# Step 0 of a matrix-state recurrence, prepared inside the matrix product before it

## Chip, cores and metric

The kernel runs on one core of one Trainium2 chip. The metric is the device time of one execution in microseconds (us), as the median of several runs.

## What is computed

A trunk of two layers on 512 tokens of width 1024, in float32. Layer 0 has a gated mixer (gMLP), layer 1 an RWKV-7 time mixer; a squared-ReLU MLP and a LayerNorm follow each. The change lies in the time mixer of layer 1. Its projections come first, then a recurrence over tokens with a 64x64 state per head:

```python
r = xr @ w_rkv[0]
k = xk @ w_rkv[1]
v = xv @ w_rkv[2]
...
def step(state, inp):
    r_t, w_t, k_t, v_t, kk_t, b_t = inp
    sa = jnp.einsum('bhij,bhj->bhi', state, -kk_t)
    state = (state * w_t[:, :, None, :] + sa[..., None] * b_t[:, :, None, :]
             + v_t[..., None] * k_t[:, :, None, :])
    y = jnp.einsum('bhij,bhj->bhi', state, r_t)
    return state, y
```

The kernel doesn't run it token by token. It takes 128 tokens of 8 heads at once (a step), turns the decays into cumulated exponents, and gets the effect of the tokens in a step on each other from 128x128 products (the grams) and a triangular inverse.

## The kernel before

**Engines.** Five programs are written out by hand, one for each engine, and meet only in semaphores. Each engine works in the order in which its program is written, so an instruction that waits holds all that stands behind it.

**Products.** A float32 weight slab of 128 rows (`raw`) is split in two parts, `w_hi` by ScalarE and `w_lo` by POOL (GpSimd); the tokens likewise in `a_hi` (ScalarE) and `a_lo` (VectorE). `row_tile(j, t, ...)` does one slab `j` (one of 4 slots) for one token tile `t` (one of 4): six matmul instructions into banks 2t and 2t+1 of PSUM. `row_product` runs eight slabs: the first four slab by slab, the last four with the token tile as the outer loop, so that tile 0 is finished first and ScalarE can evict it (`projected`, by way of `stage` to the DRAM tensor `proj`) while the others are summed. `tile_summed` and `slab_used` tell of finished tiles and slabs, `proj_read` of evicted banks. The projections run in the order key, receptance, value. The sigmoids, keys and receptances of the first tokens come back from `proj` to `early` while the value product runs; the values (`late`) come after it.

**The recurrence.** Eight steps, each a pair of token tile and half of the heads (`Step(i)`). For each of them come, in this order: scaling and norm of kk; `log_decays` (TensorE: one product with the triangle `cumulate` into bank CUM, four with `halves` into bank HALVES); `decay_before` (VectorE: the exponent p_prev); `decays_of` (ScalarE: four exponentials); `decay_ab` and `decay_kr` (VectorE: four token products into `tok_ar` and `tok_bk`); `turn_ab` and `turn_rk` (TensorE: 16 transposes into four banks GRAM); `turned_pairs` (ScalarE: copies to `turned4`); `interactions(n, g)` (TensorE: the grams, in two halves g, into the same banks); `mask_grams` (VectorE: eight masks into `gram`); and then `iteration`, in which the inverse of step q is built while the state passes step s = q - 1 and step n = q + 1 is prepared. Step 0 has nothing to be prepared in: before, its preparation stands between the value product and the first `iteration`. On POOL, `scale_k` and `bonus_terms` prepare the keys and the bonus (`rk`).

**Memory.** The buffers of the recurrence lie over those of the products: `gram`, `inverse` and `k_rest` over weight slots and operands, `start` over an end of `big`. So `inverse` and `k_rest` can only be written when the value product is done; VectorE waits for that with `slab_used`, then clears `inverse`, makes `k_rest` and clears `start` (semaphore `zeroed`), and builds `select`, `terms` and a column of `block_inv` from the identity.

Of the kernel before, what the change touches and what calls it, by code (L numbers as in the profile page):

```python
# [6 lines left out]
P = 128  # L7
# [45 lines left out]
def trunk(nc, x, ln1_g, ln1_b, ln2_g, ln2_b, ffn_w1, ffn_w2, gm_w_in, gm_vn_g, gm_vn_b, gm_ws, gm_bs,  # L53
# [7 lines left out]
    HALF = D // 2  # L61
# [34 lines left out]
    with ExitStack() as ctx:  # L96
# [92 lines left out]
        turned4 = over("turned4", [P, 2, PAIRS, 4, P])  # L189
        kkn, scratch, k_gain = (over(name, [P, HALF]) for name in ("kkn", "scratch", "k_gain"))  # L190
# [83 lines left out]
        GRAM = (2, 3, 5, 6)  # L274
        TURN_BANK = (0, 1, 4, 5, 6, 0, 1, 7)
# [114 lines left out]
        def _(pool):  # L390
# [164 lines left out]
        def _(act):  # L555
# [183 lines left out]

            products = ("key", "receptance", "value")  # L740
# [12 lines left out]
            for u, name in enumerate(products):  # L753
# [11 lines left out]
                for t in range(TT):  # L765
# [8 lines left out]
                    projected(3 + u, t, ACT.Copy)  # L774


            def decays_of(n):

                act.wait_ge(lx_ready, n.nth(1, 1))
                nc.scalar.activation(decays[:, n.i % 3], bank[HALVES][:, 0:2 * PAIRS].rearrange("p (a b) -> p a b", b=2),  # L780
                                     ACT.Exp).then_inc(exp_ready, 1)
                nc.scalar.activation(p_prev[:], p_prev[:], ACT.Exp).then_inc(exp_ready, 1)
                nc.scalar.activation(p_inv[:], bank[CUM][:], ACT.Exp, scale=-1.0).then_inc(exp_ready, 1)
                nc.scalar.activation(p_mid[:], bank[CUM][:], ACT.Exp).then_inc(exp_ready, 1)
# [35 lines left out]
            def copy_corner(q):  # L820

                act.wait_ge(level_summed, q.nth(6, 6))
                if q.i >= 2:
# [47 lines left out]
            def turned_pairs(n):  # L871
                for p in range(PAIRS):
                    act.wait_ge(turned_summed, n.nth(PAIRS, p + 1))
                    nc.scalar.activation(turned4[:, n.half, p].rearrange("p a t -> p (a t)"), bank[GRAM[p]][:],
                                         ACT.Copy).then_inc(turned_ready, 1)

# [984 lines left out]
```

## Time and profile before

| | |
|---|---|
| median of 3 runs | 1432.93 us (1430.86 to 1434.05) |
| the profiled execution | 1430.15 us, span 1428.4 us |
| TensorE (PE) | busy 1342.5 us, 94% of the span |
| VectorE (DVE) | 675.5 us, 47% |
| ScalarE (ACT) | 512.0 us, 36% |
| GpSimd (POOL) | 589.3 us, 41% |
| mean granted clock of TensorE | 0.963 |

The busy shares are averages over the whole kernel. The value product ends at about 733 us and the recurrence lies between there and about 1010 us; the rest is products. The profiled execution is not one of the three runs of the median.

### The profile page before, as it was taken

Reading aid. Unit: us, or ns where it says so; the run is one execution under the profiler, and the core shown is the slowest. Engines: PE = TensorE matmul, PEld = TensorE weight load, DVE = VectorE, ACT = ScalarE, POOL = GpSimd, SP = SyncE. Lnnn points to the kernel's source line nnn. Section 1 sums busy time; section 2 is a strip of 40 time slices with the busy share of each in tenths; the row PEclk is TensorE's granted clock in tenths of the full one; section 3 lists DMA queues with packets and bytes.
Section 4 is the critical chain, followed back from the end, with each engine's and each line's share of the span. In section 5 each row is a group of like instructions: output and inputs, shape, how many; then the busy total and the mean of one; then the engine's idle time right before and its main releaser. Section 6 shows DMA issues by size and latency. Waiting matters only on the chain.

```text
span 1428.4 us, 22922 instructions
## 1 busy us (share of the span) xinstructions
PE 1342.5 (94%) x9193; PEld 1087.4 (76%) x9193; DVE 675.5 (47%) x871; ACT 512.0 (36%) x879; POOL 589.3 (41%) x356
## 2 busy tenths in 40 slices
PE   7989999999999979999977999998799999999996
PEld 6878888888888852477755888777678888888885
DVE  2475811112444485146647677772582111244447
ACT  4443232223232321433433666765323322323230
POOL 4344344444444450134524354553344444344440
PEclk9999999999999989999988989998899999999999
DMA  7224243333443330534531111101234333233321
GB/s 265 74 74 133 74 120 101 93 97 103 130 124 97 98 102 16 193 116 148 177 133 31 32 46 47 46 20 59 84 107 120 102 91 100 77 114 103 91 71 59
DMA packets 108974, 138.22 MB, mean 97 GB/s; under 512 B 6162, under 2 KB 81986, under 8 KB 108900
## 3 DMA queue, kind: packets, MB, share of 16 engines
q1 hardware_dynamic: 104292, 120.37, 28.0%
q10 hardware_dynamic: 4608, 16.78, 3.1%
q8 instruction: 56, 0.92, 0.3%
q14 instruction: 18, 0.15, 0.0%
HBM read 122.45 MB, written 14.68 MB: 96 GB/s over the span
## 4 chain that ended last, share of the span: by engine, by line
PE 76%; DVE 17%; ACT 4%; issue 2%; POOL 0%; DMA 0%; ACTq 0%; SPq 0%; DVEq 0%; POOLq 0%
PE bank L1402 35%; PE bank L1455 8%; PE bank L1454 8%; PE bank L1456 8%; DVE a_lo L983 3%; PE bank L1547 2%; PE bank L1564 2%; DVE gram L1263 2%; DVE x_tok L1011 2%; DVE x_tok L1009 2%; PE bank L1753 1%; DVE stats L1000 1%; PE bank L1637 1%; DVE x_tok L1026 1%; DVE v_tok L1011 1%
## 5 line engine op out<-in xcount | busy, mean ns | idle before, releaser
L397 POOL TENSOR_TENSOR w_lo<-raw,w_hi 128x1024 fp32r<-128x1024 f32 x184 | 454.9, 2478 | 644.7 <-ACT w_hi L569 636.7
L569 ACT ACTIVATE w_hi<-raw 128x1024 fp32r<-128x1024 f32 x184 | 193.6, 1056 | 292.2 <-PE bank L1402 280.5
L1402 PE MATMUL bank<-w_hi,a_hi 128*128 128x512 f32 x896 | 280.3, 394 | 16.1 <-DVE a_lo L983 11.0
L1402 PE MATMUL bank<-w_lo,a_hi 128*128 128x512 f32 x896 | 277.6, 391 | 0.0
L1402 PE MATMUL bank<-w_hi,a_lo 128*128 128x512 f32 x896 | 277.0, 390 | 0.0
L1454 PE MATMUL bank<-xT_hi,w_hi 128*128 128x512 f32 (+1 forms) x640 | 236.1, 369 | 0.0
L1455 PE MATMUL bank<-xT_lo,w_hi 128*128 128x512 f32 (+1 forms) x640 | 235.5, 368 | 0.0
L1456 PE MATMUL bank<-xT_hi,w_lo 128*128 128x512 f32 (+1 forms) x640 | 235.4, 368 | 0.0
L983 DVE TENSOR_TENSOR a_lo<-big,a_hi 128x512 fp32r<-128x512 f32 x64 | 140.6, 2202 | 182.6 <-ACT a_hi L588 179.5
L1402 PEld LDWEIGHTS bank<-w_hi,a_hi 128*128 128x128 f32 x896 | 166.8, 189 | 57.6 <-issue 16.0
L1402 PEld LDWEIGHTS bank<-w_lo,a_hi 128*128 128x128 f32 x896 | 169.1, 189 | 35.7
L1402 PEld LDWEIGHTS bank<-w_hi,a_lo 128*128 128x128 f32 x896 | 168.9, 189 | 35.7
L1092 DVE TENSOR_TENSOR big<-relu 128x512 f32 (+1 forms) x64 | 45.6, 712 | 274.6 <-ACT relu L696 274.6
L1454 PEld LDWEIGHTS bank<-xT_hi,w_hi 128*128 128x128 f32 x640 | 120.7, 189 | 20.1
L1456 PEld LDWEIGHTS bank<-xT_hi,w_lo 128*128 128x128 f32 x640 | 120.7, 189 | 20.1
L1455 PEld LDWEIGHTS bank<-xT_lo,w_hi 128*128 128x128 f32 x640 | 120.7, 189 | 19.5
L696 ACT ACTIVATE relu<-bank 128x512 f32<-128x512 f32 x64 | 38.4, 600 | 236.2 <-PE bank L1456 236.2
L983 DVE TENSOR_TENSOR a_lo<-mix,a_hi 128x512 fp32r<-128x512 f32 x24 | 43.1, 1795 | 83.4 <-ACT a_hi L744 83.4
L1263 DVE TENSOR_TENSOR gram<-bank,keep_before 128x512 f32<-128x512 f32 x64 | 39.0, 680 | 15.7 <-PE bank L1617 15.7
L727 ACT ACTIVATE stage<-bank 128x512 f32<-128x512 f32 x48 | 26.0, 594 | 55.6 <-PE bank L1402 40.5
L473 POOL COPY inverse<-grown 32x256 f32<-32x256 f32 x32 | 17.3, 539 | 62.1 <-issue 35.4
L1617 PE MATMUL bank<-turned 64*128 64x256 f32 x256 | 39.3, 409 | 0.0
(219 smaller groups left out, 1435.0 us busy)
## 6 DMA issues: line engine op xcount, KB each, us to landing
raw<-in_ffn_w SPq DMA_DIRECT2D x128, 512.0 KB, 3.9
raw<-in_rw_w_rkv SPq DMA_DIRECT2D x24, 512.0 KB, 3.6
proj<-stage ACTq DMA_DIRECT2D x24, 512.0 KB, 2.6
raw<-in_gm_w_in SPq DMA_DIRECT2D x16, 512.0 KB, 4.3
early<-proj SPq DMA_DIRECT2D x8, 1024.0 KB, 6.1
raw<-in_gm_w_out SPq DMA_DIRECT2D x8, 512.0 KB, 3.6
raw<-in_rw_w_o SPq DMA_DIRECT2D x8, 512.0 KB, 3.5
late<-proj SPq DMA_DIRECT2D x8, 512.0 KB, 3.9
```

The lines of the kernel that those rows point to most:

```text
L397: nc.gpsimd.tensor_tensor(w_lo[:, j, :], raw[:, j, :], w_hi[:, j, :].bitcast(F32), ALU.subtract).then_inc(w_lo_ready, 1)
L569: nc.scalar.activation(w_hi[:, j, :], raw[:, j, :], ACT.Copy).then_inc(w_hi_ready, 1)
L696: nc.scalar.activation(relu[:, j % 2, :], bank[j][:], ACT.Relu).then_inc(bank_read, 1)
L983: nc.vector.tensor_tensor(a_lo[:, j, :], source(i * SLOTS + j), a_hi[:, j, :].bitcast(F32), ALU.subtract).then_inc(a_lo_ready, 1)
L1011: nc.vector.scalar_tensor_tensor(y, y, rstd[:, 0:1], gains[:, 1, :], ALU.mult, ALU.add).then_inc(result, 1)
L1092: nc.vector.tensor_tensor(big[:, i * SLOTS + j, :], relu[:, j % 2, :], relu[:, j % 2, :], ALU.mult).then_inc(squared, 1)
L1263: nc.vector.tensor_tensor(gram[:, n.half, h:h + 3:2, 2 * g:2 * g + 2, :], bank[GRAM[b]][:].rearrange("p (e a t) -> p e a t", e=2, a=2), ke ...
L1402: last = nc.tensor.matmul(bank[2 * t + h][:], a[:, j, tok], w[:, j, h * HALF:(h + 1) * HALF], start=start and a is a_hi and w is w_hi, sto ...
L1454: nc.tensor.matmul(dst, w_hi[:, j, col], xT_hi[:, k, tokens], start=k == 0, stop=False)
L1455: nc.tensor.matmul(dst, w_hi[:, j, col], xT_lo[:, k, tokens], start=False, stop=False)
L1456: last = nc.tensor.matmul(dst, w_lo[:, j, col], xT_hi[:, k, tokens], start=False, stop=k == KT - 1)
L1617: last = nc.tensor.matmul(bank[GRAM[b]][:, p % 2 * 2 * P:(p % 2 + 1) * 2 * P], turned4[r, n.half, p, (B_, K_)[g], :], turned4[r, n.half, p ...
```

## The change

Step 0 of the recurrence is prepared inside the value product. `row_product` calls a function `between(t, j)` after each row tile of its last four slabs, and for the value product TensorE does there: the log decays after row tile (1,0), `turn_ab` after (2,1), `turn_rk` after (2,3), the first half of the grams after (3,1), and the second after (3,3), the last. For step 0 the banks differ: 0 and 1 for the decays and 0 to 3 for transposes and grams, which are the banks of token tiles 0 and 1, once they have been evicted. ScalarE gets the exponentials behind the eviction of tile 0 and the copies of turned pairs behind that of tile 2; VectorE masks the first half before it waits for the end of the value product. Since `p_prev`, `p_inv` and `p_mid` lie over memory that the product still uses, step 0 has three buffers of its own in the second half of `turned4`. `k_rest` and the clearing of `start` and `inverse` go to POOL, which waits for the end of the value product; TensorE now waits for `zeroed` ahead of the first `iteration` and no longer ahead of the transposes. Waits for the last stores to `proj` go to where a buffer that lies over `stage` is first written (`copy_xa`, `centre_y`).

```diff
+        p_prev0, p_inv0, p_mid0 = (sb(name, [P, HALF], at=place["turned4"] + (PAIRS * 4 * P + m * HALF) * 4)
+                                   for m, name in enumerate(("p_prev0", "p_inv0", "p_mid0")))
...
+        def gram_banks(n):
+            return GRAM if n.i else (0, 1, 2, 3)
+
+        def decay_banks(n):
+            return (CUM, HALVES) if n.i else (0, 1)
+
+        def exponents(n):
+            return (p_prev, p_inv, p_mid) if n.i else (p_prev0, p_inv0, p_mid0)
...
             scale_k(Step(0))
+
+            pool.wait_ge(slab_used, first_slab["rw_out"])
+            then(nc.gpsimd.tensor_scalar(k_rest[:], k_a[:], -1.0, 1.0, ALU.mult, ALU.add))
+            then(nc.gpsimd.memset(start[:], 0.0))
+            nc.gpsimd.memset(inverse[:], 0.0).then_inc(zeroed, 1)
             for z in range(2):
...
                     projected(3 + u, t, ACT.Copy)
+                    if name == "value" and t == 0:
+                        decays_of(Step(0))
+                    if name == "value" and t == 2:
+                        turned_pairs(Step(0))
...
             def copy_xa(s):
+                if s.i == 0:
+                    for z in range(2):
+                        act.wait_ge(stage_out[z], 16 * 6 * TT // 2)
...
-            decays_of(Step(0))
-            for z in range(2):
-                act.wait_ge(stage_out[z], 16 * 6 * TT // 2)
-            turned_pairs(Step(0))
             steps(iteration)
...
             decay_kr(first_step)
+            mask_grams(first_step, 0)
 
             dve.wait_ge(slab_used, first_slab["rw_out"])
-            then(nc.vector.memset(inverse[:], 0.0))
-            then(nc.vector.tensor_scalar(k_rest[:], k_a[:], -1.0, 1.0, ALU.mult, ALU.add))
-            nc.vector.memset(start[:], 0.0).then_inc(zeroed, 1)
             then(nc.vector.tensor_reduce(select[:], ident[:].rearrange("p (m j) -> p j m", j=BASE), AX.X, ALU.add))
             for c in range(BASE):
                 here = select[:, c:c + 1].broadcast_to([P, HH])
                 then(nc.vector.tensor_copy(terms[:, :, c, c], here))
                 if c == 0:
                     then(nc.vector.tensor_copy(block_inv[:, :, 0], here))
-            for z in range(2):
-
-                dve.wait_ge(stage_out[z], 16 * 6 * TT // 2)
-            mask_grams(first_step)
+            mask_grams(first_step, 1)
             steps(iteration)
...
+            def within_value(t, j):
+
+                if (t, j) == (1, 0):
+                    pe.wait_ge(masks_ready, 1)
+                    pe.wait_ge(proj_read, 8 * 5 + 2)
+                    log_decays(first_step)
+                if (t, j) == (2, 1):
+                    pe.wait_ge(proj_read, 8 * 5 + 4)
+                    turn_ab(first_step)
+                if (t, j) == (2, 3):
+                    turn_rk(first_step)
+                if (t, j) == (3, 1):
+                    interactions(first_step, 0)
+                if (t, j) == (3, 3):
+                    interactions(first_step, 1)
+            for u, name in enumerate(("key", "receptance", "value")):
+                row_product(name, KT, None, lambda t: pe.wait_ge(proj_read, 8 * (u + 2) + 2 * t + 2),
+                            between=within_value if name == "value" else None)
...
-            pe.wait_ge(proj_read, 8 * 5 + 6)
-            log_decays(Step(0))
             pe.wait_ge(proj_read, 8 * 6)
             pe.wait_ge(zeroed, 1)
-            turn_ab(Step(0))
-            turn_rk(Step(0))
-            interactions(Step(0), 0)
-            interactions(Step(0), 1)
             steps(iteration)
```

On ScalarE, from the last operands of the value product on, before (stage is the eviction, turned_101 is `turned4`):

```order
L738 ACTIVATE small<-small 128x8 [waits ss_ready]
L727 ACTIVATE stage<-bank 128x512 [waits stage_out0,tile_summed]
L727 ACTIVATE stage<-bank 128x512
L730 DMA proj<-stage 128x1024 [waits proj_read]
L727 ACTIVATE stage<-bank 128x512 [waits stage_out1,tile_summed]
...
L780 ACT_TABLE_LOAD
L780 ACTIVATE decays<-bank 128x8 [waits lx_ready]
...
L874 ACTIVATE turned_101<-bank 128x512 [waits turned_summed,stage_out1,stage_out0]
L874 ACTIVATE turned_101<-bank 128x512 [waits turned_summed] x3
```

and now:

```order
L754 ACTIVATE small<-small 128x8 [waits ss_ready]
L743 ACTIVATE stage<-bank 128x512 [waits stage_out0,tile_summed]
L743 ACTIVATE stage<-bank 128x512
L746 DMA proj<-stage 128x1024 [waits proj_read]
L761 ACT_TABLE_LOAD
L761 ACTIVATE decays<-bank 128x8 [waits lx_ready]
...
L770 ACTIVATE turned_101<-bank 128x512 [waits turned_summed] x4
L743 ACTIVATE stage<-bank 128x512 [waits stage_out1,slab_used]
```

The exponentials have moved ahead of the evictions of tiles 1 to 3, and the copies of turned pairs ahead of that of tile 3.

On VectorE, from the last token product of step 0 to its masks, before:

```order
L1207 TENSOR_TENSOR tok_ar<-early,p_mid 128x512 [waits exp_ready]
L1347 MEMSET inverse 128x1024 [waits slab_used]
L1348 TENSOR_SCALAR k_rest<-k_a 128x1024 [waits dve_done]
L1349 MEMSET start 128x1024 [waits dve_done]
L1350 TENSOR_REDUCE select<-ident 128x8
L1353 COPY terms<-select 128x8 [waits dve_done]
L1355 COPY block_inv<-select 128x8 [waits dve_done]
L1353 COPY terms<-select 128x8 [waits dve_done] x7
L1263 TENSOR_TENSOR gram<-bank,keep_before 128x2x256 [waits stage_out1,gram_summed,stage_out0,dve_done]
L1263 TENSOR_TENSOR gram<-bank,keep_before 128x2x256 [waits gram_summed] x7
```

and now (the last group is the second half of the masks):

```order
L1229 TENSOR_TENSOR tok_ar<-early,p_mid_104 128x512 [waits exp_ready]
L1289 TENSOR_TENSOR gram<-bank,keep_before 128x2x256 [waits gram_summed] x4
L1375 TENSOR_REDUCE select<-ident 128x8 [waits slab_used]
L1378 COPY terms<-select 128x8 [waits dve_done]
L1380 COPY block_inv<-select 128x8 [waits dve_done]
L1378 COPY terms<-select 128x8 [waits dve_done] x7
L1289 TENSOR_TENSOR gram<-bank,keep_before 128x2x256 [waits gram_summed,dve_done]
L1289 TENSOR_TENSOR gram<-bank,keep_before 128x2x256 [waits gram_summed] x3
```

The three large instructions have left VectorE, and half of the masks stand ahead of the wait for the last slab. On POOL the three stand now between the last product of `scale_k` and the first of `bonus_terms`:

```order
L502 TENSOR_TENSOR early<-early,k_gain 128x512 [waits k_linked]
L557 TENSOR_SCALAR k_rest<-k_a 128x1024 [waits slab_used]
L558 MEMSET start 128x1024 [waits pool_done]
L559 MEMSET inverse 128x1024 [waits pool_done]
L517 TENSOR_TENSOR rk<-early 128x512 [waits early_in0,k_ready,stage_out1,stage_out0]
```

Before, the first of these was followed at once by the last.

## Rows read from the trace of the kernel before

**Rows 1.** The page: busy us, share of the span and instructions of each engine.

```profile
PE 1342.5 (94%) x9193; PEld 1087.4 (76%) x9193; DVE 675.5 (47%) x871; ACT 512.0 (36%) x879; POOL 589.3 (41%) x356
```

**Rows 2.** The chain that ended last, 714 to 760 us: start us, us, what.

```profile
732.87 1.10 ACT stage L727 x2
...
734.34 1.28 ACT L780
...
741.15 0.92 DVE inverse L1347
...
743.07 0.92 DVE start L1349
...
749.51 4.88 DVE gram L1263 x8
754.53 1.10 PE bank L1583 x2
...
756.41 0.98 PE bank L1629 x2
```

**Rows 3.** Timeline of TensorE: start us, us, what, and the idle time before it.

```profile
717.70 0.62 PE L1402 MATMUL bank<-w_hi,a_hi 128*128 128x512 f32 x2
...
732.67 1.02 PE L1583 MATMUL bank<-early,cumulate 128*128 128x512 f32 x2
733.53 0.95 PE L1585 MATMUL bank<-halves,early 128*128 128x2 f32 x8
744.09 0.45 PE L1595 MATMUL bank<-ident,tok_ar 128*128 128x128 f32 x1 [9.61 <-DVE start L1349]
...
747.66 5.51 PE L1617 MATMUL bank<-turned 64*128 64x256 f32 x32
```

**Rows 4.** Windows of TensorE: us, busy (instructions), granted clock, DMA share, GB/s.

```profile
738.00:739.00 1.00, 0.00 (x0) 0.82 0.92 190
...
748.00:749.00 1.00, 1.00 (x7) 0.56 0.08 16
749.00:750.00 1.00, 1.00 (x12) 1.00 0.00 0
...
759.00:760.00 1.00, 0.00 (x0) 0.56 0.00 0
```

**Rows 5.** Timeline of ScalarE: eviction, table load, copies of turned pairs.

```profile
717.41 1.07 ACT L727 ACTIVATE stage<-bank 128x512 f32<-128x512 f32 x2
...
734.34 1.28 ACT L780 ACT_TABLE_LOAD   x1 [0.39 <-ACT stage L727]
...
746.57 2.06 ACT L874 ACTIVATE turned<-bank 128x512 f32<-128x512 f32 x4 [9.27 <-PE bank L1603]
```

**Rows 6.** Timeline of VectorE.

```profile
719.80 1.66 DVE L1188 SCALAR_TENSOR_TENSOR scratch<-kkn,early 128x512 f32<-128x512 f32 x1
...
736.97 1.75 DVE L1199 TENSOR_TENSOR tok_bk<-scratch,p_inv 128x512 f32<-128x512 f32 x1
...
744.60 1.43 DVE L1353 COPY terms<-select 128x8 f32<-128x8 f32 x7
...
823.32 0.77 DVE L1182 TENSOR_SCALAR small<-small 128x8 f32<-128x8 f32 x1
```

**Rows 7.** Timeline of POOL at two of these places.

```profile
736.75 1.43 POOL L506 TENSOR_TENSOR rk<-early 128x512 f32<-128x512 f32 x1 [15.83 <-DMA proj<-stage]
...
822.80 1.26 POOL L509 TENSOR_TENSOR rk<-rk,r_k 128x512 f32<-128x512 f32 x1
```

**Rows 8.** A transpose at full clock (timeline), and grams of step 1 (chain).

```profile
772.76 0.28 PE L1603 MATMUL bank<-ident,tok_ar 128*128 128x128 f32 x1
772.88 0.27 PE L1603 MATMUL bank<-ident,tok_bk 128*128 128x128 f32 x1
...
773.78 1.11 PE bank L1617 x8
```

**Rows 9.** Groups of POOL's instructions: busy us, mean ns of one, idle before.

```profile
L397 POOL TENSOR_TENSOR w_lo<-raw,w_hi 128x1024 fp32r<-128x1024 f32 x184 | 454.9, 2478 | 644.7 <-ACT w_hi L569 636.7 <-PE bank L1753 8.0
...
L409 POOL TENSOR_SCALAR_AFFINE_SELECT ws_in<-ws_in 128x1024 f32<-128x1024 f32 x1 | 1.1, 1089 | 0.0
...
L423 POOL MEMSET keep_before<- 128x256 f32 x1 | 0.3, 318 | 0.0
```

**Rows 10.** Line 1182 on VectorE: ns min/median/max of its eight instructions.

```profile
L1182 DVE TENSOR_SCALAR small<-small x8: 128/130/772, 717.5 to 943.1; 128x8 f32<-128x8 f32 x8
```

More of the change, by code:

```diff
@@ L738, in norm_of, with decays_of, turned_pairs @@
                 nc.scalar.activation(small[:, NORM, :], small[:, SQ, :], ACT.Sqrt).then_inc(norm_ready, 1)
+            def decays_of(n):
+                prev, inv, mid = exponents(n)
+                cum, halves_bank = decay_banks(n)
+                act.wait_ge(lx_ready, n.nth(1, 1))
+                nc.scalar.activation(decays[:, n.i % 3], bank[halves_bank][:, 0:2 * PAIRS].rearrange("p (a b) -> p a b", b=2),
+                                     ACT.Exp).then_inc(exp_ready, 1)
+                nc.scalar.activation(prev[:], prev[:], ACT.Exp).then_inc(exp_ready, 1)
+                nc.scalar.activation(inv[:], bank[cum][:], ACT.Exp, scale=-1.0).then_inc(exp_ready, 1)
+                nc.scalar.activation(mid[:], bank[cum][:], ACT.Exp).then_inc(exp_ready, 1)
+            def turned_pairs(n):
+                for p in range(PAIRS):
+                    act.wait_ge(turned_summed, n.nth(PAIRS, p + 1))
+                    nc.scalar.activation(turned4[:, n.half, p].rearrange("p a t -> p (a t)"), bank[gram_banks(n)[p]][:],
+                                         ACT.Copy).then_inc(turned_ready, 1)
             products = ("key", "receptance", "value")
@@ L774, in _ @@
                     projected(3 + u, t, ACT.Copy)
[L777 to L784, printed above, removed]
+                    if name == "value" and t == 0:
+                        decays_of(Step(0))
+                    if name == "value" and t == 2:
+                        turned_pairs(Step(0))
             def copy_diagonal(q):
@@ L822, in copy_corner @@
                 act.wait_ge(level_summed, q.nth(6, 6))
+                act.wait_ge(zeroed, 1)
                 if q.i >= 2:
@@ L1176, in decay_before @@
                 dve.wait_ge(cum_summed, n.nth(1, 1))
-                nc.vector.scalar_tensor_tensor(p_prev[:], early[:, n.half, SIG, :], -DECAY, bank[CUM][:],
+                nc.vector.scalar_tensor_tensor(exponents(n)[0][:], early[:, n.half, SIG, :], -DECAY, bank[decay_banks(n)[0]][:],
                                                ALU.mult, ALU.add).then_inc(lx_ready, 1)
@@ L1198, in decay_ab @@
                     dve.wait_ge(s_summed, n.i - 2)
-                nc.vector.tensor_tensor(tok_bk[:, n.i % 3, 0, :], scratch[:], p_inv[:], ALU.mult).then_inc(tok_ready, 1)
+                nc.vector.tensor_tensor(tok_bk[:, n.i % 3, 0, :], scratch[:], exponents(n)[1][:], ALU.mult).then_inc(tok_ready, 1)
             def decay_kr(n):
@@ L1228, in centre_y @@
             def centre_y(s):
+                if s.i == 0:
+                    for z in range(2):
+                        dve.wait_ge(stage_out[z], 16 * 6 * TT // 2)
                 dve.wait_ge(y_summed, s.nth(1, 1))
@@ L1256, in link, with mask_grams @@
                 dve.wait_ge(base_linked, q.nth(LINKS + len(LEVELS), k))
-            def mask_grams(n):
-                for k in range(2 * PAIRS):
-                    b, g = k % PAIRS, k // PAIRS
+            def mask_grams(n, g):
+                for b in range(PAIRS):
+                    k = g * PAIRS + b
                     h = b // 2 * 4 + b % 2
@@ L1407, in row_product @@
             def row_product(name, count, turning=None, bank_free=None, split_turns=False,
-                            first_tiles=range(TT), begun=False):
+                            first_tiles=range(TT), begun=False, between=None):
                 n0, m0 = first_slab[name], first_act[name]
@@ L1441, in row_product @@
                             turn_x(turning, t - 2)
+                        if between is not None:
+                            between(t, j)
                     if t < TT - 1:
@@ L1567, in _ @@
                     last.then_inc(bank_projected, 1)
-            for u, name in enumerate(("key", "receptance", "value")):
-                row_product(name, KT, None, lambda t: pe.wait_ge(proj_read, 8 * (u + 2) + 2 * t + 2))
-            pe.wait_ge(masks_ready, 1)
             def head(ap, h):
```

28 lines of the change are left out of this document (13 added, 15 removed).

## Prediction

> **What bounds the kernel now.** I read the page first: TensorE is busy for 94% of the span [rows 1], so the kernel is matmuls with gaps, and a change that moves work pays only where it fills a gap on TensorE's path. The chain of waits, read in order of time, shows the one gap that this change can reach [rows 2]. The value product ends at 732.67, where TensorE goes over to the log decays of step 0 without a wait [rows 3]. Then the chain leaves TensorE: ScalarE's eviction, its table load and its exponential, four token products on VectorE, and then three VectorE instructions from 741.15 to 744.0 that clear two buffers and make k_rest. TensorE sits idle for 9.61 us until the last of them is done [rows 3]. After it come 16 transposes, 32 instructions of grams, and eight masks that end at 754.39, on which the log decays of step 1 wait [rows 2, 3]. So from 732.67 to 754.53 TensorE has 21.9 us, of which only 1.8 (log decays), 3.6 (transposes) and 5.5 (grams, paced by the masks) are work. I then read the engines one by one over this stretch, and the windows for the clock: the granted clock is 1.00 until 738, falls to 0.50 during the wait, stays there to 748, is back at 1.00 at 749, and falls again at about 759.5, some two microseconds into the next wait [rows 4]. The 16 transposes, from 744.09 to near 747.6 [rows 3], ran at 0.21 us apiece at the lower level.
>
> **The change, step by step.** I follow TensorE from the middle of the value product.
>
> Hook (1,0), the log decays. They stand after the first row tile of token tile 1, which ends at 717.70 [rows 3]; they write banks 0 and 1, so they wait for ScalarE's two copies of token tile 0, which end at 717.41 + 1.07 = 718.5 [rows 5]. That is a wait of 0.9 us with hand-over, a new one: ScalarE is late there because of the root and its table load. Behind it on TensorE stand all remaining row tiles. The work itself is 1.8 us (732.67 to 734.48, [rows 3]); it was on the path before too.
>
> Exponentials and token products. VectorE is free for the exponent of step 0 when scratch ends, 719.80 + 1.66 = 721.5 [rows 6], after the log decays are there (720.4). Then 0.7 us for it, four exponentials in 1.7 us (the table load of 1.28 us [rows 5] starts behind the eviction at 718.9 and is over by 720.2, hidden under the wait), and the products with p_prev, p_inv, p_inv, p_mid. They took 0.69 us alone but 1.75 where POOL's rk product ran [rows 6, 7]; POOL has nothing to do between 720.9 and the end of the value product, so I take 0.7 each, and the last is done at about 726. ScalarE is free again at 724, before token tile 1 ends at 724.4, so no eviction is late.
>
> Hook (2,1) and (2,3), the transposes. Token tile 1 ends at 717.70 + 0.9 + 1.8 + 3 x 1.36 = 724.4, two row tiles of tile 2 (eleven of them lie between 717.70 and 732.67 [rows 3], so 1.36 us each) take it to 727.2; tokens and evictions are there by 726, so no wait. Sixteen transposes at full clock, 0.12 us each as at 772.76 [rows 8], are 1.9 us in place of 3.6.
>
> Hook (3,1), the first half of the grams. It starts at 734.5. Its operands are ScalarE's four copies (2.06 us [rows 5]), which follow the eviction of tile 2 (730.9 to 732.0) and its store, and end at 734.4: a margin of 0.1 us, so up to 0.5 us may be lost here. The first eight of such instructions took 1.11 us in the next step [rows 8], so sixteen are 2.2; half of the mask-paced 5.51 [rows 3], 2.75, is the upper bound and 1.7 the lower. The four masks run under the last two row tiles.
>
> The value product thus ends at 732.67 + 0.9 + 1.8 + 1.9 + 2.2 = 739.5.
>
> After it. TensorE runs the second half of the grams (2.2 us) and is done at 741.7. Their masks stand on VectorE behind select and nine small copies, which wait for the last value slab, as POOL's three new instructions do. On VectorE these small ones took 2.1 us, from the end of start at 743.99 to 746.03, the last seven of them 1.43 [rows 2, 6]. POOL: the memsets have a row at 256 columns (0.318) and, at 1024 columns, the affine select (1.089) stands nearest [rows 9]; I take 1.0 us for a memset and 1.1 for k_rest, bounded by 0.7 (VectorE's own) and by POOL's 2.5 for a two-input product of this width [rows 9], and 3.3 us for all three with their links, from 739.6 to 742.9. This is where the two engines meet. A one-input VectorE instruction of 128x8 took 0.77 us where POOL ran a product, and its end at 824.09 is that product's (822.80 + 1.26); alone its shortest is 0.13 [rows 6, 7, 10]. The copies have the same size and also one input, in SBUF, so I take it that they are held up: about two slip in between POOL's three, and seven run after 742.9, to 744.35. Four masks of 0.61 (eight in 4.88, [rows 2]) end at 746.8, against 754.4 before. Gain so far 7.6 us. POOL's zeroed, for which TensorE now waits ahead of step 1, is there at 742.9, before the masks, so it costs nothing in itself; it would from 746.8 on.
>
> The rule behind this in the Trainium skill (SBUF — State Buffer, section "SBUF: two separate sides") is that the port pair which VectorE and GpSimd share is an exclusive lock for a whole instruction, which a VectorE instruction in a two-port mode needs against any GpSimd instruction. It speaks against this change, since it lets even a memset hold the copies; by it the masks end at 746.8, and no row of before shows a memset beside a copy.
>
> The clock. TensorE is idle from 741.7 to 746.8, 5.1 us. Before, the clock fell 4.3 us into the wait from 734.5, and about two into the one from 757.4 [rows 4], so I expect half speed when the log decays of step 1 and the replication start, which before ran at full clock from 754.53 to 757.4 [rows 2, 4]. Two pairs of 128x512 instructions (0.43 us apiece) double: 1.7 us, and the eight small ones 0 to 0.8; I take 2.1 in all. That is given back from the gain.
>
> Everything behind is moved as a whole: rk on POOL follows the store of the last value tile (before, 2.8 us from the end of the eviction, 732.87 + 1.10, to the start of rk at 736.75 [rows 2, 7]) and lies at 743.6 to 746.3, the level products on POOL have over 2 us of room, the loads of late and early have more. The sum is 7.6 - 2.1 = **5.5 us faster**. The profiled execution is 1430.15 us, which gives 1424.6; it lies 2.8 us below the median of the runs shown, so on that scale 1427.4.
>
> **Rivals** (times on the scale of the median).
> - As above, but the clock holds (the phase of the wait is luckier): 7.6 us, 1425.3. For it: the wait is new in length and place. Against it: both waits of this length in the rows lost the clock. 15%.
> - The copies aren't held up (they may not need what the 128x8 instruction needed, and the memsets read nothing). They end at 741.7, the masks at 744.1, 10.3 us earlier; rk at 743.6 then meets in_block and spread, as the 1.75 us product [rows 6] met it, and takes 0.7 back: 9.6, 1423.3, or 7.5 if the clock falls in this shorter wait. 20%.
> - The hooks stall or POOL is slow: k_rest at 2.5 us in place of 1.1 costs 1.4 more, the copies for turned 0.5, the grams 0.6; that leaves about 3 us, 1430. 11%.
> - No change within what can be told: ends above cancel further, or the time comes back in the recurrence, whose clock follows its own waits. 6%.
> - Slower, by one mechanism: the clearing on POOL. TensorE's wait for zeroed decides once the three instructions end after 746.8. With the clock's 2.1 us the gain is gone when they end at 752.3, which asks for 12.7 us in place of 3.3, or k_rest alone at 10.5 us; slower by over 0.2% needs 2.9 us more. POOL's 2.5 us for two inputs of this width [rows 9] speak against it; that no one-input arithmetic of this kind on POOL stands in the trace speaks for it. At 18 us in all it would be 5.3 us slower, 1438.2. 3%.
>
> **How the numbers follow.** The first case has 45%, with a range of its own of 1426 to 1429. A difference of 0.2% (2.9 us) is about what a measurement of this kernel can tell from none; the three runs shown spread over 3.2 us. The range reaches from the unheld copies with some luck (gain 10.4, 1422.5) to the stalled case (gain 2.7, 1430.2), and leaves out about 1 in 10 on the slow side and little on the fast. Faster by over 0.2%: 88%; within: 9%; slower: 3%.
>
> **What would show it.** In the profile after: TensorE idle by 0.9 us before the log decays at about 717.7; transposes of 0.12 us between row tiles at clock 1.00; no wait before the first grams; value ending near 739.5; POOL's k_rest, start, inverse in about 3.3 us; the small copies on VectorE, one or two of them near 1 us long; the last mask near 746.8; step 1's log decays at clock 0.50 with 0.85 us for an instruction. I am wrong if the copies end by 742 or the clock is 1.00 there (more gain), or if TensorE waits for zeroed or tokens (less).

## The result and the profile after

The changed kernel takes 1419.34 us in the median of 4 runs (1417.69 to 1421.46), the kernel before 1432.13 in the same comparison (4 runs, 1430.86 to 1434.05). The ratio is 0.9914, with a 95% interval of 0.9895 to 0.9933. That is 12.8 us, more than twice the 5.5 that was forecast, and the time lies below the range (1422.5 to 1430.2).

The page of the profiled execution (1419.39 us) begins:

```profile
span 1417.6 us, 22925 instructions
...
PE 1333.8 (94%) x9193; PEld 1078.0 (76%) x9193; DVE 674.6 (48%) x868; ACT 512.5 (36%) x879; POOL 591.5 (42%) x359
```

The number of TensorE's instructions is that of [rows 1], but their busy time is 8.7 us shorter. The work hasn't shrunk; the same instructions ran faster. This is the first sign of where most of the gain lies.

First, the place of the change. The timeline of TensorE after (columns as in [rows 3]):

```profile
719.18 1.10 PE L1604 MATMUL bank<-early,cumulate 128*128 128x512 f32 x2 [0.72 <-issue]
...
727.88 0.27 PE L1616 MATMUL bank<-ident,tok_ar 128*128 128x128 f32 x1
727.98 0.27 PE L1616 MATMUL bank<-ident,tok_bk 128*128 128x128 f32 x1
...
735.21 2.00 PE L1638 MATMUL bank<-turned 64*128 64x256 f32 x16
740.12 2.00 PE L1638 MATMUL bank<-turned 64*128 64x256 f32 x16
748.27 2.05 PE L1604 MATMUL bank<-early,cumulate 128*128 128x512 f32 x2 [6.15 <-DVE gram L1289]
750.11 1.71 PE L1606 MATMUL bank<-halves,early 128*128 128x2 f32 x8
751.68 2.05 PE L1671 MATMUL bank<-spread,keep_block 128*128 128x512 f32 x2
```

This execution reached the value product 0.6 us later than the one of before. Less that, the value product ends at 739.5, as worked out: a wait of 0.72 us, transposes at 0.11 us apiece, no wait ahead of the first grams, whose sixteen instructions took 2.0 us. Then TensorE waits 6.15 us for the masks, and the log decays and the replication (the product of spread, the last row above) run at half speed (0.50 granted, the 1.2 GHz level): 5.5 us from 748.27 to the end of the replication, where before it was 2.9 [rows 2]. VectorE and POOL in this wait:

```profile
736.37 2.48 DVE L1289 TENSOR_TENSOR gram<-bank,keep_before 128x512 f32<-128x512 f32 x4 [10.37 <-PE bank L1638]
...
740.65 0.71 DVE L1378 COPY terms<-select 128x8 f32<-128x8 f32 x1
741.39 0.98 DVE L1380 COPY block_inv<-select 128x8 f32<-128x8 f32 x1
742.41 3.20 DVE L1378 COPY terms<-select 128x8 f32<-128x8 f32 x7
745.64 2.48 DVE L1289 TENSOR_TENSOR gram<-bank,keep_before 128x512 f32<-128x512 f32 x4
```

```profile
740.28 1.04 POOL L557 TENSOR_SCALAR k_rest<-k_a 128x1024 f32<-128x1024 f32 x1 [18.82 <-PE bank L1424]
741.39 0.96 POOL L558 MEMSET start<- 128x1024 f32 x1
742.40 0.96 POOL L559 MEMSET inverse<- 128x1024 f32 x1
...
744.11 1.26 POOL L517 TENSOR_TENSOR rk<-early 128x512 f32<-128x512 f32 x1 [0.75 <-DMA proj<-stage]
745.44 1.28 POOL L520 TENSOR_TENSOR rk<-rk,r_k 128x512 f32<-128x512 f32 x1
```

Read the ends against each other: the copy of 741.39 ends at 742.37, when start is cleared (742.35). The next waits for inverse (743.36), and one more for rk (745.37). The two memsets and the product hold the copies alike, each one copy: four of the nine took 0.7 to 1.1 us, the other five 0.17 to 0.18. The last mask ends at 748.12, and the replication of step 0 starts at 751.68 in place of 756.27, 4.6 us earlier. Only that much is won here.

The rest comes later. A step lasts from one replication (line 1629 before, 1671 after) to the next; below are these distances as worked out from the starts of the replication's rows, and in brackets the time at half clock within each (a low stretch is a time at half clock).

| us | step 0 | 1 | 2 | 3 | 4 | 5 | 6 | last replication |
|---|---|---|---|---|---|---|---|---|
| before | 26.85 (13.7) | 30.75 (6.8) | 30.88 (6.8) | 31.08 (6.8) | 28.16 (0) | 29.55 (3.4) | 30.70 (6.8) | 964.24 |
| after | 29.41 (21.7) | 27.93 (0) | 28.02 (0) | 29.50 (3.4) | 28.28 (0) | 29.62 (3.4) | 27.75 (0) | 952.19 |

The windows over steps 1 to 6 (columns as in [rows 4]), before and then after:

```profile
783.10:964.20 181.10, 169.35 (x3232) 0.92 0.13 38
```

```profile
781.10:952.20 171.10, 159.31 (x3233) 0.98 0.13 40
```

The same instructions, one record apart, took 10.0 us less under a granted clock of 0.98 than under 0.92. The sum, in the times of the two traces: 4.6 us up to the first replication, less 2.6 given back in step 0, which lay at half clock for 21.7 us, plus 10.0 in the six steps behind, makes 12.05 at the last replication. 1.2 of it is lost again in the products behind, so that the spans differ by 10.8. A group of instructions in step 1 shows how: the same 16 products (y_rest) lie in a low stretch before and outside one after.

```profile
792.49 3.01 PE L1753 MATMUL bank<-us,gram 128*128 128x64 f32 x16 [0.19 <-ACT us L812]
795.43 1.08 PE L1637 MATMUL bank<-grown_t,level_m 32*32 32x32 f32 x64
```

```profile
790.47 2.00 PE L1795 MATMUL bank<-us,gram 128*128 128x64 f32 x16 [0.46 <-ACT us L843]
792.39 0.75 PE L1679 MATMUL bank<-grown_t,level_m 32*32 32x32 f32 x64
```

### The profile page after: what moved, and what is told of

It is laid out like the page before. It is cut to its first block, busy times and chain, and to the rows that moved or that the text cites. A ratio compares the mean times of both kernels' runs of the same rounds, so it can differ in the third digit from the quotient of the medians.

```text
span 1417.6 us, 22925 instructions
## 1 busy us (share of the span) xinstructions
PE 1333.8 (94%) x9193; PEld 1078.0 (76%) x9193; DVE 674.6 (48%) x868; ACT 512.5 (36%) x879; POOL 591.5 (42%) x359
## 4 chain that ended last, share of the span: by engine, by line
PE 76%; DVE 17%; ACT 4%; issue 2%; POOL 0%; DMA 0%; SPq 0%; DVEq 0%; ACTq 0%; POOLq 0%
PE bank L1424 35%; PE bank L1480 8%; PE bank L1478 8%; PE bank L1479 8%; DVE a_lo L1005 3%; PE bank L1571 2%; PE bank L1588 2%; DVE gram L1289 2%; DVE x_tok L1033 2%; DVE x_tok L1031 2%; DVE stats L1022 1%; PE bank L1679 1%; PE bank L1795 1%; DVE x_tok L1048 1%; DVE v_tok L1033 1%
## 5 line engine op out<-in xcount | busy, mean ns | idle before, releaser
L484 POOL COPY inverse<-grown 32x256 f32<-32x256 f32 x32 | 17.3, 539 | 52.0 <-issue 28.2
```

## Experiments

Two theories stand against each other. **C** (clock): the steps are shorter after the change only because the low stretches fall elsewhere. **O** (order): something in the steps is released earlier, and the clock follows from it. A separate question is what holds the copies.

| kernel | median us (range, runs) | ratio to before, 95% interval |
|---|---|---|
| b_late1 | 1428.58 (1424.83 to 1430.03, 10) | 0.9978 (0.9968 to 0.9988) |
| b_late2 | 1432.85 (1431.49 to 1434.48, 10) | 1.0006 (0.9995 to 1.0018) |
| a_late1 | 1426.53 (1424.36 to 1433.21, 10) | 0.9966 (0.9948 to 0.9984) |
| a_fill | 1423.41 (1419.28 to 1431.91, 10) | 0.9938 (0.9923 to 0.9952) |
| a_again | 1424.19 (1418.64 to 1426.65, 6) | 0.9918 (0.9889 to 0.9947) |
| a_third | 1420.50 (1417.55 to 1424.41, 6) | 0.9909 (0.9887 to 0.9931) |
| b_pool | 1425.23 (1423.44 to 1429.74, 9) | 0.9941 (0.9922 to 0.9960) |
| a_dve | 1430.25 (1424.26 to 1434.53, 12) | 0.9973 (0.9952 to 0.9993) |
| a_order | 1426.51 (1417.58 to 1432.82, 12) | 0.9947 (0.9923 to 0.9971) |
| a_act | 1421.05 (1415.49 to 1426.24, 6) | 0.9922 (0.9896 to 0.9949) |
| a_act2 | 1420.67 (1410.95 to 1425.01, 6) | 0.9914 (0.9884 to 0.9945) |
| b_keep | 1429.27 (1427.48 to 1431.06, 12) | 0.9979 (0.9967 to 0.9991) |
| a_keep | 1426.52 (1424.88 to 1430.21, 12) | 0.9966 (0.9955 to 0.9977) |
| b_pool_keep | 1425.99 (1424.05 to 1429.58, 6) | 0.9947 (0.9926 to 0.9968) |
| a_dve_keep | 1426.51 (1424.26 to 1427.66, 6) | 0.9948 (0.9928 to 0.9968) |
| a_act2_keep | 1418.33 (1416.57 to 1419.92, 5) | 0.9890 (0.9869 to 0.9912) |

The kernel before had medians of 1431.97 to 1433.47 in these comparisons, over 11 to 31 runs each.

### A later start: b_late1, b_late2, a_late1

In b_late1 one more memset stands ahead of step 0's transposes, in b_late2 two:

```diff
             then(nc.vector.memset(inverse[:], 0.0))
+            then(nc.vector.memset(inverse[:], 0.0))
```

> The kernel before with one more memset of inverse (0.9 us, about 1.0 with its link) ahead of step 0's transposes, so that the whole recurrence starts 1.0 us later. Theory C (clock): the 7 to 8 us that the changed kernel gained between the first and the last step come from where the stretches at half clock fall in the steps. Then this delay doesn't simply add: the steps after the first change from their 30.7 to 31.1 us to some other length between 27.8 and 31, and the time can come out several us away from +1, likely below 1432. Theory O (order): the changed kernel's steps are shorter because something in them is released earlier (loads of early and late, POOL). Then this kernel keeps steps of about 30.8 us and is 1.0 us slower than before: ratio 1.0007.

> As b_late1 with two more memsets, about 2.0 us. Theory O: +2.0 us, ratio 1.0014, steps of 30.8 us. Theory C: not additive; with the shift of 1.4 us between the changed kernel's second step and a return of the same place of the clock, this or b_late1 should lose the lock of a low stretch in each step, with steps near 28 us and a time up to 7 us below before.

```diff
+            for _ in range(4):
+                then(nc.vector.memset(in_block[:], 0.0))
             mask_grams(first_step, 1)
```

> The changed kernel with four small memsets (128x256, together about 1.1 us) on VectorE ahead of the second half of step 0's masks. Theory O: 1.1 us slower than the changed kernel, 1420.4, steps as in it (27.8 to 29.6 us). Theory C: not additive; step lengths change, the time can lie anywhere between 1418 and 1428.

More work gave 4.1 us less (b_late1 against the 1432.68 of its comparison), then nothing (b_late2). In a_late1 the four memsets took 1.5 us, not 1.1, and the changed kernel became 2 to 7 us slower (against its three medians; 7 to 8 us by the ratios to before). b_late1 speaks against O, whose +1.0 us lies outside its interval; b_late2's interval holds both O's 1.0014 and no change, and a_late1 is only clearly above O's value against two of the three medians. In b_late1 steps 3 to 6 took 28.6, 29.5, 28.2 and 29.2 us in place of 31.1, 28.2, 29.6 and 30.7; b_late2 has the lengths of before within about 0.1 us in its steps 1 to 6. I had expected b_late2 too to lose the pattern, and it didn't; the regular return in the clock that its expectation supposes is borne out by no run. The delays weren't the round ones either: counted from the first matmul of the value product, the first replication came 0.6 us later than before in b_late1 and 2.75 us later in b_late2, where it ran at half clock.

### Idle products in the wait: a_fill

```diff
+            pe.wait_ge(early_in[1], 16)
+            for _ in range(6):
+                nc.tensor.matmul(bank[Y_BANK][:], ident[:], early[:, 1, SIG, :], start=True, stop=True)
             pe.wait_ge(zeroed, 1)
             steps(iteration)
```

> The changed kernel with six idle products (ident by early, 128x512 in float32, 0.86 us each at full clock, into a bank that isn't used yet) on TensorE between the evicted last tile and the log decays of step 1, where it waits 6.15 us for the masks. Nothing of the result uses them. Both theories: the clock is 1.00 at these log decays, which with the replication take 2.7 us in place of 5.5, so the local gain grows by 2.5 to 3 us. Theory O: the total falls by the same, to 1416.5. Theory C: the total moves by that and by whatever the steps behind do, so it may differ from 1416.5 by several us either way.

The first replication came at 748.5 in place of 751.7, as both theories said, but the total didn't fall: 0.9938 of before, where the changed kernel has 0.9909 to 0.9918. Its profiled execution, the slowest of the ten at 1431.91 us, had five steps running of 30.7 to 31.1 us with 6.8 us at half clock each.

### The changed kernel again: a_again, a_third

> The changed kernel once more, unedited, for its spread: its first four runs lie between 1417.7 and 1421.5. Theory C (clock): where the low stretches fall differs from one execution to the next, so more runs reach up to about 1430, with a median up to 5 us above 1419.3. Theory O (order): all runs within 2 us of 1419.3.

> The changed kernel unedited, a third set of runs. If its clock is better than that of before on average: median 1419 to 1424, about 10 us below before, in this set too. If the first sets were lucky: a median within 5 us of before, 1427 or more.

Sixteen runs in three comparisons lie between 1417.55 and 1426.65, with medians of 1419.3, 1424.2 and 1420.5. a_third's steps are those of the table above within about 0.1 us. a_again's trace is another: the same program, with the same 62.8 us from the first matmul of the value product to the first replication, took 176.9 us for steps 1 to 6, with 6.8 us at half clock in steps 1 and 4 (30.9 and 31.1 us) and 3.4 in steps 3 and 6. So the runs vary with the clock's pattern, as C says, and not with the order. The good pattern is the changed kernel's usual one (eleven of the sixteen runs lie at 1421.7 or below, the other five at 1423.9 to 1426.7), and the gain of about 12 us (9 in a_again's comparison) is no accident of the first four.

The traces without idle products in the steps say the same together. Their 78 steps 1 to 6, of both kernels and their variants, took 30.3 to 31.1 us with 6.8 us at half clock (37 steps), 29.1 to 29.8 with 3.4 (16) and 27.8 to 28.4 with none (21); only four steps 3 without one took 28.6 to 29.2. The length follows the low stretches, whichever the kernel.

The runs give a second estimate of the clock's share, since each has its mean granted clock. At 0.964, for instance, the changed kernel has three at 1423.9 to 1424.5, and before has three of 1429.3 on average. A straight line with one slope through the 16 runs of the changed kernel and the 91 of before puts the changed kernel 5.7 us lower at the same clock (standard error 0.4); the rest of the 12 goes with its higher clock, 0.968 against 0.961.

### Idle products in every step: b_keep, a_keep

```diff
+            def idle_product(q):
+                nc.tensor.matmul(bank[GRAM[3]][:], ident[:], gram[:, q.half, 0].rearrange("p a t -> p (a t)"),
+                                 start=True, stop=True)
...
                 level_left(q, 0)
                 if s:
+                    idle_product(q)
                     u_bottom(s)
+                    idle_product(q)
```

> The kernel before with two idle products (128x512 in float32, 0.86 us each, into a bank that is free there) in each of the seven later iterations, around u_bottom, ahead of the place where its low stretches begin. They change no result. They cost at most 1.7 us a step. Theory C: if they are enough to keep the clock, steps 2 to 8 have no low stretch and take 28 + 1.7 = 29.7 us each or less, all alike, so the seven steps take about 208 us as without them, and the time is within 3 us of before. Theory O: steps stay at 30.8 us and grow by up to 1.7: the seven steps take 216 to 220 us, 8 to 12 us slower.

> The changed kernel with the same two idle products per iteration. Theory C: its steps are then as long as those of b_keep, with or without, and the difference of the two kernels is what the change brought up to the first replication, 4 to 5 us. Theory O: the changed kernel's steps stay shorter than b_keep's by 1 us or more each and the difference is 10 to 13 us.

These two decide. The windows over steps 1 to 6 of b_keep, and then of a_keep:

```profile
783.70:959.30 175.60, 168.89 (x3257) 1.00 0.13 39
```

```profile
779.90:955.60 175.70, 168.61 (x3256) 1.00 0.13 39
```

There is no low stretch in either, and they take 175.6 and 175.7 us: where the clock holds, the change did nothing to these steps. b_keep's six steps are 5.5 us shorter than before's 181.1 although they hold twelve products more; a_keep's are 4.6 us longer than the changed kernel's 171.1. The kernels differ by 2.75 us in the median (by 2.3 in the mean of 12 runs each, with a standard error of 0.6), and by 3.7 in the two traces at the last replication: 6.4 at the first (756.8 and 750.4), less 2.6 in step 0 (26.85 and 29.44 us, with 13.7 and 21.8 at half clock, where no idle product stands). Of the 6.4, 1.2 is no gain: a_keep's execution reached the value product that much earlier. From there on it is 5.2 at the first replication, as in the changed kernel, and 2.5 at the last. O is refuted. I had expected a difference of 4 to 5; it is less, since step 0 takes part of it back.

### What holds the copies: a_dve, b_pool, a_order, a_act

a_dve moves the three clearing instructions back to VectorE, ahead of select. b_pool is the kernel before with them on POOL, behind `scale_k(Step(0))`, and with a wait of ScalarE for zeroed in `iteration`.

> The changed kernel with the clearing back on VectorE, ahead of select and the copies (2.8 us there), nothing of it on POOL. Held-up theory (POOL's three instructions and rk hold the small copies): the seven copies take 1.4 us again in place of 3.2, but 2.8 us of clearing are before them, so the last mask ends at most 0.6 us earlier or later than in the changed kernel (748.1): moving the clearing to POOL brought nothing by itself. Rival (the copies are slow for another reason, such as the buffers' place): the seven copies stay at 3.2 us and the last mask ends 2.8 us later. The median differs from the changed kernel's by whatever the clock does, up to 5 us.

> The kernel before with only the clearing moved to POOL, where in the changed kernel it stands. The transposes wait for zeroed and for the last token product (741.0 before), no longer for VectorE's clearing (744.0). POOL clears from about 733 to 736, under the exponentials, so the transposes start at 741.2 in place of 744.1 and the first replication 2.9 us earlier, at 753.4, if select and the copies don't hold the masks. Theory C: median anywhere from 1425 to 1433, since the steps behind depend on the clock; theory O: 1429.8.

The seven copies in a_dve and POOL beside them, and the seven in b_pool:

```profile
744.52 3.44 DVE L1377 COPY terms<-select 128x8 f32<-128x8 f32 x7
...
744.68 1.26 POOL L517 TENSOR_TENSOR rk<-early 128x512 f32<-128x512 f32 x1 [22.64 <-DMA proj<-stage]
746.02 1.28 POOL L520 TENSOR_TENSOR rk<-rk,r_k 128x512 f32<-128x512 f32 x1
```

```profile
741.87 1.44 DVE L1355 COPY terms<-select 128x8 f32<-128x8 f32 x7
```

In a_dve the numbers are near the rival's: the copies took 3.44 us without a clearing on POOL, and the last mask ended at 750.5, 2.4 us later than in the changed kernel, of which 0.6 is a later arrival at the value product. But the reason isn't the buffers' place: being later, the copies ran into rk (POOL, 744.68 to 747.30), which my expectation had left out. In b_pool the clearing (733.04 to 736.12) and rk (to 739.97) are over before the copies, and they took 1.44. The same buffers, so their place is out: POOL work beside the copies holds them, clearing or not, and where POOL is quiet they are quick. b_pool's first replication starts at 752.05, 0.4 us behind the changed kernel's 751.68 (0.9 from the value product on), with one of the change's parts.

a_order puts the second half of the masks ahead of select and the copies behind spread and the scaling of kk:

```diff
+            mask_grams(first_step, 1)
             dve.wait_ge(slab_used, first_slab["rw_out"])
             then(nc.vector.tensor_reduce(select[:], ident[:].rearrange("p (m j) -> p j m", j=BASE), AX.X, ALU.add))
-            for c in range(BASE):
...
-            mask_grams(first_step, 1)
             steps(iteration)
```

> The changed kernel with another order on VectorE: the second half of step 0's masks first, then the wait for the last value slab and select, and the nine small copies behind spread and the scaling of step 1's kk. The masks no longer stand behind the copies that POOL holds. The last mask ends about 4 us earlier (744 in place of 748.1), the log decays of step 1 start after 2 us of idle time in place of 6.15 and run at full clock, and the first replication starts between 746.5 and 749 in place of 751.7. Theory O: 3 to 5 us faster than the changed kernel. Theory C: the first replication moves so, the median by that and up to 5 us either way.

Masks end at 743.9 and the log decays of step 1 start at 744.04 at full clock, as expected. But the nine copies now lie beside the level products and `scale_k` and take 5.7 us, and step 0 took 35.2 us in place of 29.4. It was also at half clock for 27.3 us in place of 21.7; how much of the 5.8 us is the copies' and how much the clock's isn't told apart. The traced execution (1419.57) is one of the fast ones; the median is 1426.5. The last seven copies:

```profile
749.33 4.31 DVE L1342 COPY terms<-select 128x8 f32<-128x8 f32 x7
```

a_act gives the copies to ScalarE, with select made early:

```diff
+            def fill_terms():
+                act.wait_ge(select_ready, 1)
+                for c in range(BASE):
+                    here = select[:, c:c + 1].broadcast_to([P, HH])
+                    last = nc.scalar.activation(terms[:, :, c, c], here, ACT.Copy)
+                    if c == 0:
+                        last = nc.scalar.activation(block_inv[:, :, 0], here, ACT.Copy)
+                last.then_inc(terms_ready, 1)
...
                 copy_diagonal(q)
+                if q.i == 0:
+                    fill_terms()
```

> The changed kernel with select made early on VectorE and the nine small copies (terms, block_inv) on ScalarE behind the diagonals of step 0, where ScalarE waits. VectorE has nothing between the two halves of the masks. Held-up theory (any instruction of POOL holds such copies on VectorE): the copies take 0.2 us or less apiece on ScalarE though POOL runs beside them, the last mask ends near 743.9 and the first replication starts at 746 to 747 as in a_order, but the second follows after 27 to 30 us and not after 35. Rival (the copies are slow wherever they stand): they take over 3 us on ScalarE too. Total: 4 to 5 us below the changed kernel (1424 in the call before), by what the clock adds or takes, up to 5 us.

ScalarE's copies in a_act:

```profile
743.05 0.22 ACT L908 ACTIVATE terms<-select 128x8 f32<-128x8 f32 x1
743.17 0.20 ACT L910 ACTIVATE block_inv<-select 128x8 f32<-128x8 f32 x1
743.27 0.79 ACT L908 ACTIVATE terms<-select 128x8 f32<-128x8 f32 x7
```

They followed each other every 0.1 us. POOL's clearing had ended by then (742.95), but its rk product ran from 743.69 to 744.96, beside the last three of them, and they took 0.20 us like the others: the rival that they are slow anywhere is out, and a product on POOL doesn't hold them on ScalarE. That a memset on POOL wouldn't is not shown. The first replication starts at 745.6, and step 0 is 27.5 us long. The profiled execution then had 6.8 us at half clock in five of its six steps 1 to 6, which took 182.7 us in place of the changed kernel's 171.1, more than had been won. The median, 0.9922 of before, is no better than the changed kernel's.

### Apart from the clock: a_act2, b_pool_keep, a_dve_keep, a_act2_keep

a_act2 is a_act with `(t, j) == (1, 1)` in place of `(1, 0)` for the log decays; the kernels with keep have the idle products of b_keep.

> As a_act, and the log decays of step 0 stand one row tile later, behind (1,1). The wait of 0.72 us ahead of them goes away, tokens are ready 1.4 us later but before (2,1). The value product ends 0.7 us earlier than in a_act, with everything behind it, if the copies of turned pairs still end in time: total 0.7 us below a_act apart from the clock.

> b_pool (only the clearing moved to POOL) with the two idle products per iteration. In the profile of b_pool the first replication came 4.2 us earlier than before. If its step after that is as long as before's, the time is 1425 to 1426, level with a_keep (1426.5) or below it, and the clearing alone is worth as much as the whole change apart from the clock. If its first step is longer because the clock is low in it, 1428.

> a_dve (hooks in the value product, clearing on VectorE) with the idle products. Its first replication came 2.3 us later than the changed kernel's. Its first step was shorter, 27.5 against 29.4, so I expect 0 to 2.5 us above a_keep: 1427 to 1429.

> a_act2 (copies on ScalarE, log decays one row tile later) with the idle products. Its first replication came 7 to 8 us ahead of the changed kernel's, its first step was no longer. I expect 6 to 8 us below a_keep: 1418.5 to 1420.5, the best of this group; only 3 us if the gain is given back in the first step by the clock.

In a_act2 the log decays follow without a wait, and the first replication comes 1.3 us earlier than in a_act, counted from the first matmul of the value product. Its median is level with a_act's, and its six runs go from 1410.95, at a mean granted clock of 0.976, to 1425.01, at 0.961: 14 us in one kernel, by the clock.

Against b_keep's 1429.3, the clearing alone on POOL is worth 3.3 us (b_pool_keep), the hooks alone (the parts of step 0's preparation inside the value product) 2.8 (a_dve_keep), both together 2.8 (a_keep). Only a_keep stands in the same comparison as b_keep; by the ratios to before they are 4.6, 4.4 and 1.9 us, so these figures are good to about 2 us. The traces, counted from the first matmul of the value product, show it more sharply. The gains at the first replication are 4.1, 3.5 and 5.2 us: they don't add, since both parts shorten the same wait and together they meet in the held copies. Step 0, partly at half clock, takes back 0.9, 3.0 and 2.6 us of them. With the copies freed and the log decays one tile later it is 10.9 us (a_act2_keep; 12.7 by the ratios), and its steps 1 to 6 run without a low stretch:

```profile
774.80:950.30 175.50, 168.63 (x3256) 1.00 0.13 39
```

a_act2_keep is faster than before, at 0.9890 (0.9869 to 0.9912). Its median is 1.0 to 5.9 us below the three of the changed kernel, but the intervals overlap (in the same comparison a_third has 0.9909, 0.9887 to 0.9931), so that it beats the changed kernel isn't shown.

## Why the prediction was wrong

**What held.** The walk through the value product came out to 0.1 us (739.5), term by term: the wait at the first hook 0.72 for 0.9, log decays 1.8, transposes 1.8 for 1.9, grams 2.0 for 2.2. The clearing on POOL took 3.1 us for 3.3 and held the copies, as the 128x8 row of [rows 6] suggested; TensorE didn't wait for zeroed. Half clock at step 1's log decays came, as forecast. (The fall at "about 759.5" in the prediction is at 759.1 by its own row [rows 4], 0.56 being the mean of that microsecond; nothing hangs on it.)

**A size that was off.** The masks ended at 747.5 (748.12 less 0.6) for 746.8: I let the copies run free from 742.9, but rk, which I had at 743.6 and only weighed for in_block and spread, holds one of them too. The forecast of 5.5 counts to the end of the first replication. There the gain was 4.3 us from the value product on: 6.9 at the masks for 7.6, less 2.6 for the clock for 2.1. (At the start of that replication, where half of the slow stretch is still to come, it was 5.2, or 4.6 by the times in the traces.)

**The step that failed** is "Everything behind is moved as a whole". I treated the recurrence as a block of fixed length that only slides. It isn't one: a step takes about 28.0, 29.5 or 30.8 us by the low stretches in it, in every kernel without idle products in the steps. Which steps have them differs between the kernels, and between executions of one kernel. This term, put at nothing, was 2.6 us given back in step 0 and 10.0 gained in steps 1 to 6; with the gain up to the first replication that made 12 us in place of 5.5. The warning stood on the page of the kernel before, in the line of the granted clock in 40 slices, of 35.7 us each:

```profile
PEclk9999999999999989999988989998899999999999
```

Most of its eights lie between 714 and 1036 us, where the recurrence is. I read the clock only in the stretch around the change [rows 4] and priced it at the two products that I followed. The sentence on the case of no change ("the time comes back in the recurrence, whose clock follows its own waits") names the mechanism, but with the wrong sign and 6%. That the kernel came out faster was forecast, and most of what was worked out is there. That the measured gain is clear of noise owes more to the clock, which the prediction hadn't foreseen, than to the part that it had worked out: in that respect the direction was right by luck.

With the low stretches of steps 1 to 6 taken out of both kernels, the change brings 2.75 us (a_keep against b_keep), just short of 0.2%. That still has the clock of step 0 in it, 8 us more at half clock than before, which takes 2.6 us back; at the same mean clock the line through the runs gives 5.7. The other 7 to 10 us of the three comparisons are the clock in the steps behind, which the changed kernel has better again and again, but which a delay of 1.6 us takes away (a_late1).

**Still open.** Why this start gives the changed kernel the good pattern more often than the start of before: shown is only that it does, over 16 runs, and that moving the start by 0.6 us (b_late1) or 1.6 us (a_late1) changes it, where 2.75 us (b_late2) leaves it as it was. The start within the program can't be all of it: a_again and a_third are the same program with different patterns, and their executions reached the value product at 687.2 and 690.0 us.

## To carry to other kernels

Where a loop of dependent small products follows the changed place, its length is not a constant: read the granted clock in each step before you say that everything behind only moves, and put the difference between a step with and one without a low stretch, times the steps, into the range. To compare two such kernels, put the same idle products into both, so that the clock is held where they stand and what is left is the change; here step 0 had none, and its clock stayed in the difference. And when work is moved to POOL, look at what VectorE does beside it: in a chain of tiny copies one is held by each POOL instruction that runs beside it (four of nine in the changed kernel), so such a chain belongs on ScalarE or into a time when POOL is quiet.

## What the runs showed of the hardware

- Two idle products of 128x512 in float32 (0.86 us each) per step removed every low stretch of six steps and made the steps 29.1 to 29.3 us long in most cases: longer than a step without low stretch (28.0), shorter than one with 6.8 us of it (30.8). The kernel before became 2.7 us faster by work that it doesn't need (0.9979, 0.9967 to 0.9991).
- TensorE was busy for 169.35 of 181.1 us in before's steps 1 to 6 by its records, and its clock fell all the same. The fall in step 1 (793.2) lay behind a stretch of 64x64 and 32x32 products (788.05 to 792.3), but the changed kernel has the same products there and its clock held, with 159.31 of 171.1 us busy. Neither the busy time in the profile nor this place tells whether the clock holds.
- A VectorE copy of eight elements a partition waits for a POOL memset, not only for a product: 0.98 us for 0.17. On ScalarE such copies took 0.20 us beside POOL's product (a_act).
